# Hybrid attention step: softmax rows normalised behind the value product, compressed scores in one bank, and ScalarE's copies and exponentials reordered

## The reference

```
def nsa_attend(q, gts, q_pos, k_cmp, v_cmp, k_sel, v_sel, k_win, v_win, win_pos, rel_bias):
    ...
    p_cmp = masked_softmax(lg, m_cmp)
    o_cmp = jnp.einsum('bghqn,bngd->bqghd', p_cmp.astype(v_cmp.dtype), v_cmp)
    ...
    o_sel = jnp.einsum('bghqnk,bgqnkd->bqghd', p_sel.reshape(shp).astype(vs.dtype), vs)
    ...
    o_win = jnp.einsum('bghqw,bwgd->bqghd', p_win.astype(v_win.dtype), v_win)
    g = jax.nn.sigmoid(gts.astype(jnp.float32)).astype(q.dtype)[..., None]
    return g[:, :, 0] * o_cmp + g[:, :, 1] * o_sel + g[:, :, 2] * o_win
```

## Time and profile before

| | us |
|---|---|
| median of 3 runs | 1687.86 |
| lowest and highest | 1687.69, 1689.75 |
| profiled execution | 1685.65 |
| its span, first to last instruction | 1683.9 |
| PE, PE weight loads, DVE, ACT, POOL busy | 1527.7, 1313.5, 750.5, 632.4, 319.7 |

### The profile page before, as it was taken

How to read it: one execution, slowest core, us unless ns; L and a number is a source line. 1 busy time by engine, 2 the same in 40 slices (tenths; PEclk the granted TensorE clock), 3 DMA queues, 4 the chain that set the end, 5 groups by cost and what they waited for, 6 DMA issues and landing times.

```text
span 1683.9 us, 25185 instructions
## 1 busy us (share of the span) xinstructions
PE 1527.7 (91%) x9970; PEld 1313.5 (78%) x9970; DVE 750.5 (45%) x1847; ACT 632.4 (38%) x1253; POOL 319.7 (19%) x380
## 2 busy tenths in 40 slices
PE   4997999999999999879949989989989989799996
PEld 1887999999999999867737757767766766588884
DVE  2541222213222132255467767767767764452231
ACT  2330111111111111134467757766766765431110
POOL 1104000000000000120024534434434441000000
PEclk8998999999999999989969989999999999899998
DMA  9708332232322323196120121011010029763320
GB/s 342 123 26 292 103 96 70 71 101 57 77 77 68 101 61 76 50 320 192 34 84 26 30 64 39 26 39 38 27 39 26 28 78 335 203 204 100 100 60 26
DMA packets 164933, 164.59 MB, mean 98 GB/s; under 512 B 48684, under 2 KB 146028, under 8 KB 159504
## 3 DMA queue, kind: packets, MB, share of 16 engines
q1 hardware_dynamic: 150800, 96.66, 21.4%
q0 software_dynamic: 14016, 66.32, 11.5%
HBM read 131.27 MB, written 35.83 MB: 99 GB/s over the span
## 4 chain that ended last, share of the span: by engine, by line
PE 81%; ACT 5%; DMA 5%; DVE 5%; issue 3%; SPq 1%; POOL 0%; DVEq 0%; ACTq 0%
PE PS L934 32%; PE PS L1257 10%; PE PS L1075 9%; PE PS L1058 7%; PE PS L1035 5%; PE PS L982 4%; PE PS L1036 3%; ACT pr L1422 2%; DMA wr<-in_w_in 2%; PE PS L896 1%; PE PS L897 1%; PE PS L898 1%; DMA adaw<-in_ada_w 1%; DMA wor<-in_w_out 1%; ACT ptt L1442 1%
## 5 line engine op out<-in xcount | busy, mean ns | idle before, releaser
L934 PE MATMUL PS<-hhi,wh 128*128 128x352 f32 x1152 | 251.5, 326 | 9.4 <-issue 8.8
L934 PE MATMUL PS<-hhi,wl 128*128 128x352 f32 x1152 | 248.7, 323 | 0.0
L934 PE MATMUL PS<-hlo,wh 128*128 128x352 f32 x1152 | 248.6, 324 | 0.0
L786 POOL TENSOR_SCALAR pr<-pr,rg 128x640 f32<-128x640 f32 (+7 forms) x128 | 204.2, 1607 | 210.0 <-DVE rg L1787 210.0
L1422 ACT ACTIVATE pr<-PS,nm 128x640 f32<-128x640 f32 (+7 forms) x256 | 179.1, 701 | 76.9 <-DVE nm L1766 74.5
L934 PEld LDWEIGHTS PS<-hhi,wh 128*128 128x128 f32 x1152 | 196.2, 190 | 13.3 <-issue 11.8
L934 PEld LDWEIGHTS PS<-hhi,wl 128*128 128x128 f32 x1152 | 198.2, 188 | 0.0
L934 PEld LDWEIGHTS PS<-hlo,wh 128*128 128x128 f32 x1152 | 196.3, 188 | 0.0
L1058 PE MATMUL PS<-ident,pr 128*128 128x128 f32 x1056 | 149.1, 276 | 8.8 <-ACT pr L1433 5.3
L1639 DVE TENSOR_TENSOR wl<-wr,wh 128x1024 fp32r<-128x1024 f32 x48 | 58.6, 1221 | 187.6 <-ACT wh L1338 187.1
L1058 PEld LDWEIGHTS PS<-ident,pr 128*128 128x128 f32 x1056 | 122.9, 142 | 21.0 <-ACT pr L1433 8.5
(11 more groups left out here) (312 smaller groups left out, 2318.5 us busy)
## 6 DMA issues: line engine op xcount, KB each, us to landing
wr<-in_w_in SPq DMA_DIRECT2D x32, 512.0 KB, 7.7
adaw<-in_ada_w SPq DMA_DIRECT2D x8, 1024.0 KB, 10.3
wr<-in_w_in SPq DMA_DIRECT2D x32, 256.0 KB, 3.7
qb<-q_stacked SPq DMA_DIRECT2D x32, 256.0 KB, 3.1
mr<-mixed SPq DMA_DIRECT2D x16, 512.0 KB, 3.9
mixed<-ych POOLq DMA_DIRECT2D x8, 528.0 KB, 3.4
z_attn_silu<-zab POOLq DMA_DIRECT2D x8, 528.0 KB, 2.9
xb<-in_x_prompt POOLq DMA_DIRECT2D x8, 512.0 KB, 8.0
```

Source lines behind the costliest of these rows:

```text
L786: ins = po.tensor_scalar(pr[r][:, h, 0:k], pr[r][:, h, 0:k], rg[:, r, h:h + 1], None, ALU.mult)
L934: ins = pe.matmul(PS[:, bank + c, 0:CH], a[kind % 2][:, k, :], b[:, k, c * CH:(c + 1) * CH], start=(k == 0 and b is hhi and a is wh), stop ...
```

## The change

Selected and window probabilities are no longer scaled. POOL widens the factors of a half (reciprocal times gate, `widen`) to 64 columns for each head. PE turns both halves' factors of a unit at the first window quarter (`turn_factors`, four blocks into one bank), and ACT copies them to `fac`. Selected and window sums now stand in separate halves of bank 6. DVE multiplies the selected sum by its factors (`selected_o`). The compressed values then go to the columns that this freed. DVE multiplies the window sum (`near_o`) and adds the compressed one to the selected one. POOL adds both and multiplies by `silu(z)` (`gate_o`). Compressed scores share the bank of the last window quarter where that has 384 keys or fewer (tiles 0 to 2). DVE makes one copy of turned blocks in four instead of one in two, ACT the rest. ACT makes only the first copy of a quarter ahead of the exponential, the second behind it. PE multiplies all held tiles of the selected half with their values in the first window quarter. The core of the diff:

```diff
-            two = keys_of(n // 4)[0] > 512 or n % 8 == 7
+            two = keys_of(n // 4)[0] > (384 if n % 8 == 7 else 512)
...
+        def cmp_bank(n):
+
+            return score_bank[n] + (keys_of(n // 4)[0] > 384)
...
+        ring0 = [0]
+        for w in range(NI):
+            ring0.append(ring0[-1] + tiles_of(w) + w % 2)
+
+        def ring(w, t):
+
+            return ring0[w] + w % 2 + t
...
+        turn_by_dve = [False] * ring0[NI]
+        for w in range(NI):
+            for t in range(tiles_of(w)):
+                turn_by_dve[ring(w, t)] = (tile0[w] + t) % 4 == 1
+
         def turned(c):
 
-            return (pt_dve if c % 2 else pt_act), c // 2 + 1
+            return (pt_dve if turn_by_dve[c] else pt_act), sum(x == turn_by_dve[c] for x in turn_by_dve[:c + 1])
...
-                    sp.wait_ge(r_ev, u - 1)
+                    sp.wait_ge(mix_rdy, u - 1)
...
+            def scale_first(u):
+
+                r, n = (2 * u + 1) % 3, 2 * unit(u)[1] + 2
+                po.wait_ge(r_rdy, factors_of(2 * u + 1) + 1)
+                po.tensor_tensor(prc[r][:, :, 0:n], prc[r][:, :, 0:n], ext(rg[:, r, 4:8], (0, n)), ALU.mult).then_inc(c_pool, 1)
+
+            def widen(w):
+
+                u = w // 2
+                i, c0_, a = unit(u)[1], head_of(u, 0), 1 + w % 2
                 po.wait_ge(r_rdy, factors_of(w))
-                for h in range(2):
-                    ins = po.tensor_scalar(pr[r][:, h, 0:k], pr[r][:, h, 0:k], rg[:, r, h:h + 1], None, ALU.mult)
-                ins.then_inc(n_pool, 1)
-                if w % 2:
-                    n = 2 * unit(w // 2)[1] + 2
-                    po.wait_ge(r_rdy, factors_of(w) + 1)
-                    po.tensor_tensor(prc[r][:, :, 0:n], prc[r][:, :, 0:n], ext(rg[:, r, 4:8], (0, n)), ALU.mult).then_inc(c_pool, 1)
+                if u:
+                    po.wait_ge(t_mm, ring0[2 * u - 1] + 1)
+                x, y = rrec[:, w % 3, 0:1], sg[:, i, NH * a + c0_:NH * a + c0_ + 1]
+                po.tensor_tensor(wide[:, w % 2, :, :].rearrange("p j (g d) -> p j g d", g=NG),
+                                 bass.AP(x.tensor, x.offset, [list(x.ap[0]), [1, 2], [2, NG], [0, HD]]),
+                                 bass.AP(y.tensor, y.offset, [list(y.ap[0]), [1, 2], [8, NG], [0, HD]]), ALU.mult).then_inc(f_rdy, 1)
+
+            def gate_o(u):
+
+                m = mixs[u % 2]
+                po.wait_ge(r_ev, u + 1)
+                po.tensor_tensor(m[:, :, :], m[:, :, :], ow[:, :, :], ALU.add).then_inc(pch, 1)
+                chain.n += 1
+                po.wait_ge(za_ld[u % 2], 16 * (u // 2 + 1))
+                po.wait_ge(pch, chain.n)
+                po.tensor_tensor(m[:, :, :], m[:, :, :], zau[u % 2][:, :, :], ALU.mult).then_inc(mix_rdy, 1)
...
-            scale(0)
-            for w in range(NI):
-                if w + 1 < NI:
-                    scale(w + 1)
-                if w % 2 and w + 2 < NI:
-                    first(w // 2 + 1)
+            widen(0)
+            for u in range(NU):
+                widen(2 * u + 1)
+                if u:
+                    gate_o(u - 1)
+                scale_first(u)
+                if u + 1 < NU:
+                    widen(2 * u + 2)
+                    first(u + 1)
+            gate_o(NU - 1)
...
-                    pe.wait_ge(n_act, w + 1)
-                    pe.wait_ge(n_pool, w + 1)
+                    pe.wait_ge(e_done, 4 * w + 4)
...
+            def turn_factors(u):
+
+                c = ring0[2 * u + 1]
+                pe.wait_ge(f_rdy, 2 * u + 2)
+                if c >= 3:
+                    pe.wait_ge(*turned(c - 3))
+                for a in range(2):
+                    for j in range(2):
+                        ins = pe.transpose(PS[:, turn_bank(c), P * (2 * a + j):P * (2 * a + j) + P], wide[:, a, j, :], ident[:, :])
                 ins.then_inc(t_mm, 1)
...
-                first, last = w % 2 == 0 and t == 0, w % 2 == 1 and t == tiles_of(w) - 1
-                if first and u:
+                pe.wait_ge(*turned(ring(w, t)))
+                cmp_ = w % 2 == 1 and t == tiles_of(w) - 1
+                if w % 2 == 0 and t == 0 and u:
                     pe.wait_ge(r_ev, u)
+                if w % 2 and t == 0:
+                    pe.wait_ge(sel_ev, u + 1)
+                a = 2 * P if w % 2 and not cmp_ else 0
+                first, last = t == 0 or cmp_, t == tiles_of(w) - 1 - w % 2 or cmp_
...
+                    if w % 2 and h == 0:
+                        turn_factors(w // 2)
                     for t in part:
                         turn_p(w, t)
...
-                    old = [x for x in held if x[0] < w - w % 2]
-                    go = len(old) if w % 2 == 0 and h < 2 else len(held) - 1 if len(held) >= 5 else 0
+                    old = [x for x in held if x[0] < w]
+                    go = len(old) if h < 2 else len(held) - 1 if len(held) >= 5 else 0
...
-            pe.wait_ge(r_ev, NU)
-            pe.wait_ge(*turned(tile0[NI] - 1))
-            pe.wait_ge(*turned(tile0[NI] - 2))
+            pe.wait_ge(mix_rdy, NU)
+            pe.wait_ge(*turned(ring0[NI] - 1))
+            pe.wait_ge(*turned(ring0[NI] - 2))
...
-            def scale(w, h):
-                k, r = keys_of(w)[0], w % 3
-                act.wait_ge(r_rdy, factors_of(w))
-                ins = act.activation(pr[r][:, h, 0:k], pr[r][:, h, 0:k], ACT.Copy, scale=rg[:, r, h:h + 1])
-                if h == 3:
-                    ins.then_inc(n_act, 1)
+            def copy_factors(u):
+                c = ring0[2 * u + 1]
+                act.wait_ge(t_mm, c + 1)
+                if u:
+                    act.wait_ge(r_ev, u)
+                act.activation(fac[:, :, :, :].rearrange("p a j c -> p (a j c)"), PS[:, turn_bank(c), :], ACT.Copy).then_inc(pt_act, 1)
...
+                        copy_factors(w // 2)
+                    for t in part[:1]:
+                        if not turn_by_dve[ring(w, t)]:
                             copy_p(w, t)
-                    if w + 1 < NI and h == 1:
-                        scale(w + 1, 2)
                     if w + 2 < NI:
                         exps(w + 2, h)
-                    if w + 1 < NI and h == 1:
-                        scale(w + 1, 3)
+                    for t in part[1:]:
+                        if not turn_by_dve[ring(w, t)]:
+                            copy_p(w, t)
...
-                    dve.wait_ge(n_act, w - 2)
-                    dve.wait_ge(n_pool, w - 2)
-                    dve.wait_ge(c_pool, (w - 2) // 2)
...
-                link(dve.reciprocal(rrec[:, r, 0:4], rsum[:, r, 0:4]))
-                dve.tensor_tensor(pairs(rg[:, r, 0:4]), pairs(rrec[:, r, 0:4]), sgh(2 if w % 2 else 1), ALU.mult).then_inc(r_rdy, 1)
+                dve.reciprocal(rrec[:, r, 0:4], rsum[:, r, 0:4]).then_inc(r_rdy, 1)
...
-            def gate_o(u):
-                dve.wait_ge(pv_mm, tile0[2 * u + 2])
-                dve.wait_ge(za_ld[u % 2], 16 * (u // 2 + 1))
+                dve.tensor_copy(pt[tc % NPT5][:, :, :], PS[:, turn_bank(c), :].rearrange("p (h c) -> p h c", h=4)).then_inc(pt_dve, 1)
+
+            def selected_o(u):
+                dve.wait_ge(pv_mm, tile0[2 * u + 1])
+                dve.wait_ge(*turned(ring0[2 * u + 1]))
                 if u >= 2:
                     dve.wait_ge(mix_st[u % 2], 16 * (u // 2))
-                dve.tensor_tensor(mixs[u % 2][:, :, :], PS[:, 6, 0:2 * P].rearrange("p (j c) -> p j c", j=2), zau[u % 2][:, :, :], ALU.mult).then_inc(r_ev, 1)
+                dve.tensor_tensor(mixs[u % 2][:, :, :], PS[:, 6, 0:2 * P].rearrange("p (j c) -> p j c", j=2), fac[:, 0, :, :], ALU.mult).then_inc(sel_ev, 1)
+
+            def near_o(u):
+                dve.wait_ge(pv_mm, tile0[2 * u + 2])
+                if u:
+                    dve.wait_ge(mix_rdy, u)
+                link(dve.tensor_tensor(ow[:, :, :], PS[:, 6, 2 * P:4 * P].rearrange("p (j c) -> p j c", j=2), fac[:, 1, :, :], ALU.mult))
+                dve.wait_ge(sel_ev, u + 1)
+                dve.tensor_tensor(mixs[u % 2][:, :, :], PS[:, 6, 0:2 * P].rearrange("p (j c) -> p j c", j=2), mixs[u % 2][:, :, :], ALU.add).then_inc(r_ev, 1)
...
-                        gate_o(w // 2 - 1)
+                        near_o(w // 2 - 1)
...
+                    if w % 2 and h == 1:
+                        selected_o(w // 2)
```

More of the change, by code:

```diff
@@ L226, in build @@
         kb0 = sb("kb0", [P, NSEL, DKV], cx=c4)
+        wide = sb("wide", [P, 2, 2, P], cx=c4)
+        ow = sb("ow", [P, 2, P], cx=c4)
         c4.close()
@@ L1042, in scores @@
                         c0_ = 384 + 2 * NPB * hh
-                        ins = pe.matmul(PS[:, b0 + 1, c0_:c0_ + 2 * NPB], qb[u % 4][:, hh, :], kcp[:, hh // 2, :], start=True, stop=True)
+                        ins = pe.matmul(PS[:, cmp_bank(n), c0_:c0_ + 2 * NPB], qb[u % 4][:, hh, :], kcp[:, hh // 2, :], start=True, stop=True)
                 ins.then_inc(s_mm, 1)
             def turn_p(w, t):
-                tc = tile0[w] + t
```

(52 more changed lines are left out.)

38 lines of the change are left out of this document (19 added, 19 removed).

## The result

The changed kernel took 1660.13 us (median of 4 runs, 1656.85 to 1665.57), the kernel before 1687.78 beside it. The ratio is 0.9846, with a 95% interval of 0.9807 to 0.9884. The profiled span fell from 1683.9 to 1654.9 us (-29.0). The forecast was 1668, a gain of 19.8: the sign held, and the gain was 8 us larger. The time lies at the lower edge of the range that the forecast itself was given (1660 to 1677), as far from 1668 as from rival 4's 1652.

A forecast was written before the change was run, and what follows sets the result against it. PE was taken to bound prompt attention, with 12.0 us idle a head group. Terms 14.1 - 30.3 - 10.3 + 6 - 1 + 2.0 = -19.5 us gave 1666 profiled, 1668 as median; range 1660 to 1677.

The forecast's parts named there:

- rival 4: More than forecast: all idle time but some 2 us a group goes, the clock returns wholly: 1652 us, chance 0.12.
- A: Added PE work in prompt attention: 32 units each turn four blocks of row factors at 0.44 us, +14.1 us.
- B: PE stalls from row scaling and the bank pair go or shrink: 7.6 us a head group, -30.3 in all.
- D: New PE waits for late ScalarE copies and for window values behind DVE's selected sum: 1.5 us a group, +6.
- F: Stage ends: first turn no longer waits for two POOL passes, -1; PE waits for DVE and POOL at the end, +2.0.
- About 0.5 of 1.37: PE's stall at 1142: the exponential moves forward by the scale pass ahead of it, saving about 0.5 us.
- the 2.02: PE stall from the bank pair, in us: only 1.0 taken as gone, since DVE sets a floor in tile 0.
- C: Clock: tile 1's half-speed stretch returns to full speed in three groups, 3 x 3.4 = -10.3 us; bounds 0 and -16.
- E: Moved copies, DVE passes and POOL's factor and output passes cost nothing; +19 us if POOL's cover went.
- Rival 1: Clock stays low in tiles 0 and 1: 1678 us, or 1685 with another stretch a group; chance 0.14.
- Rival 2: ScalarE's second copies come late, 56 waits of 0.71 us, 40 us in place of 6: 1702 us, chance 0.12.
- Rival 3: The stall passes to VectorE: its maxima hold the exponentials, halving the stall gain: 1683 us, chance 0.08.

The follow-up runs named there:

- the experiment with the passes behind: The kernel before with both of ScalarE's second-quarter scale passes moved behind the exponential: ratio 0.9958, stage 504.6 us against 518.0.
- the two-bank experiment: The changed kernel with a second bank again for the compressed scores in tiles 0 to 2: ratio 0.9928, stage 500.3 us.
- the one without the deferral: The kernel before with one bank for compressed scores and both scale passes behind the exponential, no deferred factors: 1656.94 us, ratio 0.9862, stage 486.6 us.

## Why the prediction was right, point by point

**A, the factor turns: right.** Predicted 32 x 0.44 = 14.1. The work grew by 13.5, and doubling the turns gave 0.42 each, of which 0.35 reached the stage's length. The mean over the stage (0.56) that I turned down would have given 18.

**B and D, idle time: right as a sum.** In the stage -30.3 + 6 and F's -1 stood for -25.3; measured -25.6. The parts hold less well. The one bank was to bring 3.01 x 4 = 12.0 of it; alone it brought 10.9, but taking it back from the changed kernel lost only 5.5, since there other work sets the floor. "About 0.5 of 1.37" was too much by the experiment with the passes behind (0.24), and with the deferral the 2.02 did not shrink by 1.0: two stalls of 0.34 and 1.19 stand in its place in tile 0, where DVE is full. D's late copy stands where I put it, at the end of tile 6's selected keys, at 0.91 us instead of 0.5:

```profile
1160.00 1.11 ACT L1479 ACTIVATE pr<-PS,nm 128x1024 f32<-128x1024 f32 x1 [0.55 <-DVE nm L1818]
1161.11 0.59 ACT L1499 ACTIVATE ptt<-PS 128x512 f32<-128x512 f32 x1
```

PE's turn follows at 1161.75 (the last line of its timeline above). In tile 7 there was none in this group. Where I had two of 0.5 a group there was one: 0.9 in tile 6 of the first and third group, 0.4 in tile 7 of the second and fourth. The window values waited 0.4 us for the selected sum in the whole stage, where I had 2. Waits for DVE's copies add 1.5. Together D came to 4.6 us in waits (2.7 + 0.4 + 1.5) against 6. The ordering's cost by the experiment on it was 3.6.

**C, the clock: the one mis-sized term.** Predicted -10.3 within bounds of 0 and -16, measured -19.6, outside them. The term took back tile 1's stretch and left tile 0's and the one at the start, and gave no reason for either; the floor of DVE in tile 0, under B, is one of idle time. The three groups' stretches of 10.2 us at the lower level all went and gave 15.4, and the start's, 14.7 to 6.3 us, gave 4.2. What failed is taking tile 0 to keep its low clock because it keeps idle time: it kept 1.5 us (9.60 - 8.06) and had a clock of 1.00. What sets the level there stays open. With the 1.78 us stall of the two-bank experiment tile 0 was at 0.75, with stalls of 0.34 and 1.19 at 1.00, but the run with doubled widening had stalls as short at 0.85, and the one without the deferral had 2.6 us of idle time at 1.00. So how much of the clock comes back could not have been read off the stalls, and the full return in tile 0 was in part luck.

**E, no price for POOL and the copies: right.** Factor turns never waited in the changed kernel, and the widening took 614 ns where I had estimated 0.60. The output passes took 0.73. **F**: at the start PE's wait of 0.97 us for POOL's pass (L786) is gone, as predicted (-1). At the end, +2.0 predicted, a pause of 1.7 seen:

```profile
1347.61 0.72 POOL L824 TENSOR_TENSOR mixs<-mixs,ow 128x256 f32<-128x256 f32 x1 [3.17 <-DVE mixs L1873]
1348.48 0.72 POOL L828 TENSOR_TENSOR mixs<-mixs,zau 128x256 f32<-128x256 f32 x1
...
1349.25 0.42 PE L1175 MATMUL PS<-ident,kvs 32*128 32x32 f32 x2 [2.65 <-POOL mixs L828]
```

**The sum.** The stage gave -31.7 where the terms said 14.1 - 25.3 - 10.3 = -21.5. C is 9.3 of the 10.2 between them. What the medians gained, 27.7 us, is less than the stage did.

**The rivals.** Rival 1 (the clock stays low) fell: the time at the lower level went from 45.4 to 6.3 us. The rule behind it, in the Trainium skill, "TensorE: Matmul & The Clock Gate", Part 4, that transposes don't count as busy, is neither borne out nor excluded: 128 turned blocks more, and then another 128, left that time at 6.3 and 7.7 us, so turns did no harm; but one bank alone gave 11.9 us by the clock without any added turn, so the return isn't shown to come from turns. Rival 2 (late copies) is real as a mechanism, at 3 to 4 us in place of 40. Rival 3 (VectorE) holds in tile 0 alone. Its 1683 was not counted among the faster outcomes, though it lies 4.9 us below 1687.9 and the line was drawn at 3.4; with it the chance of a faster kernel was 0.86, not 0.78. Rival 4 is what happened in its clock part (all but the 6.3 us at the start came back), not in its idle part: 21.9 us stayed, where it had some 8. Of the signs named beforehand, most held: tile 1 takes 7.2 us at 1.00, no wait for a scaled row is left, PE did not wait for the factors, and no group is longer than 124.8 us. The wait for exponentials fell to 16.0 us and not to 12, and the waits for copies came to 4.2 us and not 6.

What the forecast did not ask is which part earns the gain. It named them together under B. The experiments say that the one bank alone gives 1.4%, and that the deferral pays for its own turns and the rest could be had by moving two scale passes.

## What to carry to other kernels

Where an engine is idle at short intervals and its clock falls in the same stretches, price both, and allow for the clock to come back in the neighbouring stretch too: here it was worth 19.6 us beside 25.6 of idle time. How much comes back was not told by the length of the stalls, so give the term a wide range and read the clock of more than one profile. Before moving work to the engine that bounds, try the cheap edits of order and of buffers (one bank instead of a pair, a pass behind instead of ahead of what others wait for), since these alone reached the same time. And of copies that an in-order engine makes behind a long instruction, give the late ones to the engine that is free, rather than every fourth.

## What the runs showed of the hardware

Stalls of 1 to 2 us went with stretches at the lower clock: the bank pairs' stalls, of up to 1.80 us each, cost 5.5 us of idle time in the stage and another 7.8 by the clock. The level isn't a matter of the stalls in the tile alone: 1.5 us of idle time in tile 0 stood beside 0.85 as well as beside 1.00 in one and the same profile. A profile of one kernel differed from another by 2.8 us at the lower level. Four fp32 128x128 turned blocks cost 0.42 us among others and 0.60 alone. On POOL the same 128x256 fp32 operation took 614 ns with two operands repeated from a few values, and 734 ns with two full ones.
